# Two transformer blocks in one kernel: PSUM banks of the output products, places of split weights, order of the first splits

## The chip, the cores and the metric

The kernel runs on one core of a Trainium2 chip. The metric is device time in microseconds (us) for one launch: before the change the median of three runs is 2657.95 us (2655.5 to 2659.04). PE is TensorE (matrix products and transposes, which write to PSUM, eight banks of 128 partitions x 512 fp32 numbers), ACT is ScalarE, DVE is VectorE, POOL is GpSimd, and SP is the queue that starts the transfers from memory.

## What is computed

256 tokens of 1024 features go through four mixers, each followed by a gated feed-forward part (FFN): two layers whose mixer has three branches (mLSTM, sparse attention, differential attention), one retention mixer, one short convolution. The last FFN is a mixture of eight experts, two for each token. Cut to the parts that the change touches:

```python
# end of a layer's mixer                              (x2)
merged = gates[0] * (y_a @ w_branch[0]) + gates[1] * (y_b @ w_branch[1]) + gates[2] * (y_c @ w_branch[2])
x = x + merged @ w_out
x = x + (silu(n(x) @ w_gate) * (n(x) @ w_up)) @ w_down
# retention: four heads of 512 values
o = normed(retention(q, k, v));  x = x + (silu(g) * o) @ ret_w_out          # 2048 -> 1024
x = x + swiglu(n(x))                                                       # d_ff = 3584, "the third FFN"
# short convolution
x = x + (B * conv3(C * h)) @ conv_w_out
# experts: top 2 of 8, softmax over the two logits
x = x + sum(gate[:, e] * swiglu_e(n(x)))
out = n(x) * g
```

`n` is an RMS norm. Everything is fp32; the large products are made in fp32r from two parts each.

## The kernel before

**Products in three parts.** For a product in fp32r each operand is split in a high part (a copy rounded to fp32r) and a low part (the operand less its high part). `mm3` adds three matmuls: high x high, high x low, low x high. So each unit of weights (1 MB, 2048 numbers for each partition) that arrives in the ring of six units is read twice: ACT or POOL writes the high part (L1195, L2251), then DVE the low part (L1625, `weights_low`). For the mixers the unit is split in two halves of 1024 numbers (`half_highs` on ACT, `half_lows` on DVE, L1639). Four places hold the split halves, four places of 16 KB (`split_place`) the split units; from the retention mixer on, the halves lie in the memory of split places 0 and 1, and the retention's output inputs in places 2 and 3.

**Banks.** PE takes its PSUM banks from rotating pools, one counter for each pool: `fill(ALL)` goes round all eight, `fill(LOW)` round 0 to 3, `fill(HIGH)` round 4 to 7. `fill` waits until whoever was to empty the bank has done so, at whole banks. Pools overlap, so a bank taken from one pool may still be held by another pool's last user. `give_low` marks a bank that ACT and then DVE must read (the high and the low part of an input).

**Output products.** `to_x_split` (`merged @ w_out`, `o @ ret_w_out`, `y @ conv_w_out`) takes four banks from LOW and adds all its products there, going over 8 or 16 input tiles k. Between them stand transposes of what comes next: `turn_merged` (merged branches), `turn_o` (gated retention output), `turn_residual` (new x, for the FFN). The retention's gates are made by `chunk_split`, which takes two banks from ALL: the halves of a chunk are four steps, then ACT reads both banks with Silu (`v_or_g`). ACT works one chunk ahead in the halves: it makes the fourth half of the next chunk before it empties this chunk's banks. After each of the last three gate chunks, `turn_o(h - 1)` turns one head.

**Starts of the mixers.** `input_split` runs five filler matmuls while the norm is computed, turns the input in four banks from ALL, and runs one more filler (a product that nobody reads) in a bank from LOW, before the first product.

**Orders written by hand.** Nothing is scheduled: PE, ACT, DVE, POOL and SP each run their own list, tied by semaphores. In the third FFN POOL makes the high parts: the first unit when `turn_o(3)` has been read ("o turned"), the others when the new x is complete ("mixed"). DVE's `to_ffn` adds the products to x and makes the low parts of the FFN's inputs.

## Time and profile before

| | |
|---|---|
| Time of three runs, us | 2655.5, 2657.95, 2659.04 |
| The profiled execution, us | 2658.11, its span 2656.3 |
| PE busy | 2592.8 us, 98% of the span |
| DVE, ACT, POOL busy | 68%, 46%, 8% |
| Mean granted clock of PE | 0.994 of full speed |
| Moved by DMA | 610.13 MB, 230 GB/s |

PE is the engine that is busy nearly all the time: the time can fall only where PE waits or runs slowly, and rises by every wait that is added to it. So the profile is read by PE's waits, and for each by what stands around it in order of time. In the rows below a number in square brackets is the idle time of the engine just before the row, and the arrow what ended it; `xN` counts the recorded instructions that a row merges, and each row gives start and length in us.

### The profile page before, as it was taken

The numbers are of one execution on the slowest core, as the hardware profiler recorded it, in microseconds if no ns is written. First come the engines' busy times: TensorE is split into PE (matmuls) and PEld (weight loads), VectorE is DVE, ScalarE is ACT, GpSimd is POOL, SyncE is SP. The second block draws the span as 40 slices with busy tenths as digits, with TensorE's granted clock in tenths as the row PEclk, the third lists the DMA queues.
The fourth block names the chain that finished last, engine by engine and source line by source line (L and its number), as shares of the span: only waits on it lengthen the run. The fifth ranks groups of instructions, "written<-read, shape, count | busy, mean of one in ns | idle before, by whom it ended". The sixth has DMA issues, their size and how long they took to land.

```text
span 2656.3 us, 29239 instructions
## 1 busy us (share of the span) xinstructions
PE 2592.8 (98%) x11620; PEld 1989.4 (75%) x11620; DVE 1803.0 (68%) x1953; ACT 1226.1 (46%) x1423; POOL 218.8 (8%) x104
## 2 busy tenths in 40 slices
PE   8999999999999999999999998999999999999997
PEld 5455578865555888977788897878787888888886
DVE  3754555447445554745655567999999999999996
ACT  2233220023323102363100346777787877777775
POOL 0000023200000332000433100000000000000000
PEclk9999999999999999999999998999999999999999
DMA  6342455534334555545555455999999989999995
GB/s 214 129 154 100 158 192 189 170 110 137 127 113 170 193 190 173 184 157 175 175 190 190 143 176 181 375 325 381 320 379 325 377 324 376 325 355 347 354 345 188
DMA packets 273636, 610.13 MB, mean 230 GB/s; under 512 B 10476, under 2 KB 47522, under 8 KB 273338
## 3 DMA queue, kind: packets, MB, share of 16 engines
q1 hardware_dynamic: 273466, 607.67, 64.6%
q8 instruction: 131, 2.15, 0.3%
q14 instruction: 39, 0.32, 0.0%
HBM read 606.58 MB, written 1.05 MB: 229 GB/s over the span
## 4 chain that ended last, share of the span: by engine, by line
PE 90%; DVE 6%; ACT 3%; issue 1%; DMA 0%; SPq 0%; DVEq 0%; ACTq 0%
PE bank L467 87%; DVE split L1625 4%; PE bank L709 1%; PE bank L497 1%; ACT split L1195 1%; ACT parts L1195 0%; ACT xs L1195 0%; DVE tmp L1674 0%; DVE parts L1686 0%; ACT pbuf L1195 0%; DMA pbuf<-in_gain_rows 0%; DVE parts L1613 0%; ACT L1195 0%; ACT halves L1195 0%; DVE ybuf_tmp_high L1639 0%
## 5 line engine op out<-in xcount | busy, mean ns | idle before, releaser
L467 PE MATMUL bank<-split,parts 128*128 128x512 f32 (+1 forms) x6432 | 1463.3, 388 | 5.7 <-DVE split L1625 3.1
L467 PEld LDWEIGHTS bank<-split,parts 128*128 128x128 f32 x6432 | 1189.4, 188 | 247.3 <-issue 4.0
L1625 DVE TENSOR_TENSOR split<-ring,split 128x2048 fp32r<-128x2048 f32 x444 | 1020.4, 2344 | 81.9 <-POOL split L2251 60.9
L1195 ACT ACTIVATE split<-ring 128x2048 fp32r<-128x2048 f32 x344 | 659.6, 1921 | 187.0 <-PE bank L467 187.0
L467 PE MATMUL bank<-ring,xnT 128*128 128x512 f32 (+2 forms) x896 | 367.6, 567 | 0.0
L2251 POOL TENSOR_SCALAR split<-ring 128x2048 fp32r<-128x2048 f32 x100 | 218.6, 2187 | 1265.2 <-PE bank L467 1035.9
L467 PEld LDWEIGHTS bank<-ring,xnT 128*128 128x128 f32 x896 | 169.4, 190 | 180.0 <-issue 178.9
L1195 ACT ACTIVATE parts<-bank 128x512 fp32r<-128x512 f32 x128 | 68.8, 590 | 327.4 <-PE bank L709 327.4
L1639 DVE TENSOR_TENSOR halves<-ring,halves 128x1024 fp32r<-128x1024 f32 x96 | 116.4, 1224 | 84.1 <-ACT halves L1195 83.5
L1195 ACT ACTIVATE halves<-ring 128x1024 fp32r<-128x1024 f32 x96 | 101.3, 1059 | 153.9 <-PE bank L467 153.9
L1686 DVE TENSOR_TENSOR parts<-bank,parts 128x512 fp32r<-128x512 f32 x128 | 82.4, 686 | 124.9 <-ACT parts L1195 124.9
L1195 ACT ACTIVATE z<-bank 128x512 f32<-128x512 f32 (+2 forms) x52 | 29.6, 568 | 234.2 <-PE bank L467 234.2
L467 PEld LDWEIGHTS bank<-xparts,halves 128*128 128x128 f32 x960 | 115.5, 190 | 2.1 <-ACT xparts L1195 1.6
L467 PE MATMUL bank<-xparts,halves 128*128 128x256 f32 x960 | 116.1, 284 | 0.8 <-DVE xparts L1613 0.8
L1676 DVE SCALAR_TENSOR_TENSOR tmp<-bank,xsum,tmp 128x512 f32<-128x512 f32 (+1 forms) x38 | 27.5, 723 | 110.9 <-PE bank L467 110.9
L1195 ACT ACTIVATE tmp<-bank,xsum 128x512 f32<-128x512 f32 (+1 forms) x38 | 25.3, 667 | 141.6 <-PE bank L467 141.5
L467 PE MATMUL bank<-halves,xparts 128*128 128x512 f32 x384 | 88.6, 391 | 0.0
L467 PE MATMUL bank<-ring,ybuf 128*128 128x512 f32 x192 | 84.1, 594 | 3.5 <-ACT ybuf L1195 3.5
L467 PEld LDWEIGHTS bank<-halves,xparts 128*128 128x128 f32 x384 | 71.8, 188 | 15.1 <-issue 0.5
L1660 DVE TENSOR_TENSOR x_resid<-bank,x_resid 128x512 f32<-128x512 f32 x60 | 41.1, 691 | 51.1 <-PE bank L467 51.1
L1674 DVE TENSOR_TENSOR tmp<-bank,tmp 128x512 f32<-128x512 f32 x112 | 72.6, 685 | 0.2
L467 PEld LDWEIGHTS bank<-ring,ybuf 128*128 128x128 f32 x192 | 35.8, 190 | 46.5 <-issue 42.1
(260 smaller groups left out, 1861.1 us busy)
## 6 DMA issues: line engine op xcount, KB each, us to landing
ring<-in_moe_w_gate SPq DMA_DIRECT2D x112, 1024.0 KB, 8.0
ring<-in_moe_w_up SPq DMA_DIRECT2D x112, 1024.0 KB, 7.5
ring<-in_moe_w_down SPq DMA_DIRECT2D x112, 1024.0 KB, 7.5
ring<-in_w_gate_up SPq DMA_DIRECT2D x44, 1024.0 KB, 5.8
ring<-in_w_in SPq DMA_DIRECT2D x40, 1024.0 KB, 7.1
ring<-in_ret_w_in SPq DMA_DIRECT2D x24, 1024.0 KB, 5.1
ring<-in_w_down SPq DMA_DIRECT2D x22, 1024.0 KB, 5.1
ring<-in_w_in SPq DMA_DIRECT2D x20, 880.0 KB, 6.5
```

What stands on the lines that cost most here:

```text
L467: return nc.tensor.matmul(o, l, r, start=first, stop=final, **kw)
L497: ins = nc.tensor.transpose(bank[b][:, i * P:i * P + rows], src_of(i), ident[0:rows, 0:rows])
L709: return [nc.tensor.transpose(bank[b[tt]][:, f * P:(f + 1) * P], hb[:, tt, f * P:(f + 1) * P], ident) for f in range(n // P)]
L1195: return nc.scalar.activation(out, in_, func, **kw)
L1625: V.tensor_tensor(split[:, split_place(m), 1, :], ring[:, n % RING, :], split[:, split_place(m), 0, :].bitcast(F32), ALU.subtract).then_in ...
L1639: V.tensor_tensor(low, half_of(n, j, by_column), high.bitcast(F32), ALU.subtract).then_inc(half_low.sem, half_low.tick())
L1660: ins = V.tensor_tensor(o, b[:, :], o, ALU.add)
L1674: ins = V.tensor_tensor(hb[:, tt, 0:n], b[:, 0:n], sg[:, tt, 0:n], ALU.mult)
L1676: ins = V.scalar_tensor_tensor(hb[:, tt, 0:n], b[:, 0:n], xsum[:, 3, tt:tt + 1], sg[:, tt, 0:n], ALU.mult, ALU.mult)
L1686: V.tensor_tensor(low, b[:, 0:n].rearrange("p (f t) -> p f t", t=P), high.bitcast(F32), ALU.subtract).then_inc(hidden_low.sem, 1)
L2251: nc.gpsimd.tensor_scalar(split[:, split_place(m), 0, :], ring[:, n % RING, :], 1.0, 0.0, ALU.mult, ALU.add).then_inc(high_made.sem, high_ ...
```

## The change

It has five parts. (1) Pools: `turn_merged(0)` takes its banks from LOW (was ALL), the four products of the third branch from HIGH (was ALL), every `turn_o` from HIGH (was ALL, but for the last). (2) Places: the second unit of the third FFN goes to place 0, whose halves are moved by two so that the last two halves of the retention lie in place 1; POOL makes that unit's high part as soon as two halves before the last two are read, and DVE makes the low part between the second pair of additions and the second half's input lows, instead of behind them. (3) At the end of a layer the halves and the FFN's first units are made in the order 2 halves, unit, half, unit, half, unit, unit, instead of one by one. (4) Three filler matmuls stand ahead of the last expert's `combine`. (5) Since the pools' counters advance differently, later banks from ALL and HIGH are others than before, also in code that the diff does not touch.

```diff
--- before
+++ after
@@ -44,6 +44,7 @@
 LAYER_HALVES = DEPTH * KT
+RET_HALVES = 8 * 2 + 8 * 4 + 2 * KT
 EARLY = 4
@@ -337,12 +338,17 @@
+        def half_place(h):
+            return (h if h < LAYER_HALVES + RET_HALVES else h + 2) % HALVES
         def place_half(h, by_column):
...
             else:
-                whole = [halves[:, h % HALVES, i, :] for i in range(2)]
+                whole = [halves[:, half_place(h), i, :] for i in range(2)]
             return [w.rearrange("p (k c) -> p k c", k=KT) for w in whole] if by_column else whole
@@ -370,7 +376,7 @@
                 return m % SPLITS
-            return (3, 2, 0, 1)[(m - (DEPTH * layer_splits if m < dense_splits else dense_splits)) % SPLITS]
+            return (3, 0, 1, 2)[(m - (DEPTH * layer_splits if m < dense_splits else dense_splits)) % SPLITS]
@@ -417,8 +423,8 @@
-                half_free.extend(split_read[max(m for m in range(n_split[0]) if split_place(m) == h // 2)]
-                                 for h in range(HALVES))
+                half_free.extend(split_read[max(m for m in range(n_split[0]) if split_place(m) == half_place(h) // 2)]
+                                 for h in range(n_half[0], n_half[0] + HALVES))
@@ -862,7 +868,7 @@
                     eng.wait_ge(mrg_dve.sem, pe.next(mrg_dve))
-                    turn_input(xs, (2 * h, 2 * h + 1), HIGH if h else ALL)
+                    turn_input(xs, (2 * h, 2 * h + 1), HIGH if h else LOW)
@@ -871,7 +877,7 @@
                                 turn_merged(0)
-                            b = fill(ALL)
+                            b = fill(HIGH if br == 2 else ALL)
                             for k in range(4):
@@ -1037,11 +1043,11 @@
-            def turn_o(h, pool=ALL):
+            def turn_o(h):
...
                 for fp in (2 * h, 2 * h + 1):
-                    transposes(lambda i: rv[:, i % 2, (2 * fp + i // 2) * P:(2 * fp + i // 2 + 1) * P], 4, "act", pool)
+                    transposes(lambda i: rv[:, i % 2, (2 * fp + i // 2) * P:(2 * fp + i // 2 + 1) * P], 4, "act", HIGH)
                     point("input")
@@ -1053,7 +1059,7 @@
                 if k == 4:
-                    turn_o(RH - 1, HIGH)
+                    turn_o(RH - 1)
                     point("o turned")
@@ -1135,6 +1141,7 @@
+                filler(3 if ends else 0)
                 eng.wait_ge(act_freed.sem, pe.point("y", act_freed))
@@ -1445,9 +1452,10 @@
                     half_highs(1)
-                for _ in range(EARLY):
-                    half_highs(1)
+                for n in (2, 1, 1):
+                    half_highs(n)
                     expert_high(1, layer_splits * li)
+                expert_high(EARLY - 3, layer_splits * li)
                 nth_split[0] += layer_splits - EARLY
@@ -1661,9 +1669,10 @@
-            def to_ffn(gain):
+            def to_ffn(gain, units=0):
                 for h in range(2):
                     add_to_x(BY_HALF[2 * h:2 * h + 2])
+                    weights_low(units if h else 0)
                     lows(gain, pairs=(2 * h, 2 * h + 1))
@@ -2051,9 +2060,10 @@
                 half_lows(1)
-                for _ in range(4):
-                    half_lows(1)
+                for n in (2, 1, 1):
+                    half_lows(n)
                     weights_low(1)
+                weights_low(EARLY - 3)
                 to_ffn(G_FFN + 8 * li)
@@ -2128,8 +2138,7 @@
             weights_low(1)
-            to_ffn(G_FFN0)
-            weights_low(1)
+            to_ffn(G_FFN0, 1)
             norm_inverse()
@@ -2257,8 +2266,12 @@
             weights_high(1, first)
+            for h in range(LAYER_HALVES + RET_HALVES - HALVES, LAYER_HALVES + RET_HALVES - 2):
+                sig, value = half_read[h]
+                eng.wait_ge(sig.sem, value)
+            weights_high(1, first)
             eng.wait_ge(dve_freed.sem, pool.point("mixed", dve_freed))
-            weights_high(units_of(groups2) - 1, first)
+            weights_high(units_of(groups2) - 2, first)
```

**Retention, the end of the second gate chunk on PE** (before, then changed; each row is the line, the instruction, its bank and operands, the size, what it waits for and how many like it; `halves,xparts` are the chunk's products, `const,ret_v` the transposes of `turn_o(0)`, and the rows after them the next chunk).

```order
L467 MATMUL bank7<-halves,xparts 128x512 [waits half_unit_low]
L467 MATMUL bank7<-halves,xparts 128x512 x5
L467 MATMUL bank0<-halves,xparts 128x512 x6
L497 MATMUL bank1<-const,ret_v 128x128 [waits act_emptied,retention_scaled]
L497 MATMUL bank1<-const,ret_v 128x128 x3
L497 MATMUL bank2<-const,ret_v 128x128 [waits act_emptied]
L497 MATMUL bank2<-const,ret_v 128x128 x3
L467 MATMUL bank3<-halves,xparts 128x512 [waits half_unit_low,act_emptied]
L467 MATMUL bank3<-halves,xparts 128x512 x5
```

Changed:

```order
L473 MATMUL bank3<-halves,xparts 128x512 [waits half_unit_low]
L473 MATMUL bank3<-halves,xparts 128x512 x5
L473 MATMUL bank4<-halves,xparts 128x512 x6
L503 MATMUL bank4<-const,ret_v 128x128 [waits act_emptied,retention_scaled]
L503 MATMUL bank4<-const,ret_v 128x128 x3
L503 MATMUL bank5<-const,ret_v 128x128 [waits act_emptied]
L503 MATMUL bank5<-const,ret_v 128x128 x3
L473 MATMUL bank5<-halves,xparts 128x512 [waits act_emptied,half_unit_low,inputs_low]
L473 MATMUL bank5<-halves,xparts 128x512 x5
```

Before, the transposes stood in banks 1 and 2, with nothing of the chunks around them. Now their first bank is 4, the chunk's second, and the next chunk's first bank is 5, which holds the second set of transposes. At `turn_o(1)` it is the same with banks 6 and 7. Behind `turn_o(2)` the output product used to take banks 0 to 3 with the transposes in 1 and 2; now they are in 4 and 5.

**Start of the retention mixer on PE** (`const 128x512` is filler, `const,xs` are the transposes of the input, `xparts,halves` the first product).

```order
L497 MATMUL bank6<-const,xs 128x128 [waits dve_emptied]
L497 MATMUL bank6<-const,xs 128x128 x3
L497 MATMUL bank7<-const,xs 128x128 [waits dve_emptied]
L497 MATMUL bank7<-const,xs 128x128 x3
L497 MATMUL bank0<-const,xs 128x128 [waits hidden_low,act_emptied]
L497 MATMUL bank0<-const,xs 128x128 x3
L467 MATMUL bank3<-const 128x512 [waits dve_emptied]
L467 MATMUL bank1<-xparts,halves 128x256 [waits half_unit_low,inputs_low,hidden_low,act_emptied]
L467 MATMUL bank1<-xparts,halves 128x256 x5
```

Changed:

```order
L503 MATMUL bank1<-const,xs 128x128 x3
L503 MATMUL bank2<-const,xs 128x128 x4
L503 MATMUL bank3<-const,xs 128x128 [waits dve_emptied]
L503 MATMUL bank3<-const,xs 128x128 x3
L503 MATMUL bank4<-const,xs 128x128 [waits dve_emptied]
L503 MATMUL bank4<-const,xs 128x128 x3
L473 MATMUL bank3<-const 128x512 [waits inputs_low,act_emptied]
L473 MATMUL bank5<-xparts,halves 128x256 [waits inputs_low,half_unit_low,dve_emptied]
L473 MATMUL bank5<-xparts,halves 128x256 x5
```

The filler's bank is 3 in both, but the transposes have moved from 5, 6, 7, 0 to 1, 2, 3, 4, so that the filler now waits for the third set. At the start of the convolution they move from 3, 4, 5, 6 to 1, 2, 3, 4 with the same filler in bank 3.

**Third FFN's start on DVE** (`x_resid` are the additions to x, `parts` the low parts of the FFN's input, `split` a unit's low part).

```order
L1660 TENSOR_TENSOR x_resid<-bank2,x_resid 128x512 [waits bank_for_dve]
L1660 TENSOR_TENSOR x_resid<-bank3,x_resid 128x512 [waits bank_for_dve]
L1613 SCALAR_TENSOR_TENSOR parts<-bank4,gcol,parts 128x256 [waits act_emptied,dve_emptied]
L1613 SCALAR_TENSOR_TENSOR parts<-bank4,gcol,parts 128x256
L1613 SCALAR_TENSOR_TENSOR parts<-bank5,gcol,parts 128x256 [waits act_emptied]
L1613 SCALAR_TENSOR_TENSOR parts<-bank5,gcol,parts 128x256
L1625 TENSOR_TENSOR split<-ring,split 128x2048 [waits weights_high]
L1577 TENSOR_TENSOR xsum<-xhalf 128x2 [waits squares_summed]
L1568 TENSOR_SCALAR xsum<-xsum 128x2 [waits dve_step]
L1573 RECIPROCAL xsum<-xsum 128x2 [waits root]
```

Changed:

```order
L1668 TENSOR_TENSOR x_resid<-bank2,x_resid 128x512 [waits bank_for_dve]
L1668 TENSOR_TENSOR x_resid<-bank3,x_resid 128x512 [waits bank_for_dve]
L1633 TENSOR_TENSOR split<-ring,split 128x2048 [waits weights_high,dve_emptied]
L1621 SCALAR_TENSOR_TENSOR parts<-bank6,gcol,parts 128x256 [waits act_emptied]
L1621 SCALAR_TENSOR_TENSOR parts<-bank6,gcol,parts 128x256
L1621 SCALAR_TENSOR_TENSOR parts<-bank7,gcol,parts 128x256 [waits act_emptied]
L1621 SCALAR_TENSOR_TENSOR parts<-bank7,gcol,parts 128x256
L1585 TENSOR_TENSOR xsum<-xhalf 128x2 [waits squares_summed]
L1576 TENSOR_SCALAR xsum<-xsum 128x2 [waits dve_step]
L1581 RECIPROCAL xsum<-xsum 128x2 [waits root]
```

The second unit's low part has moved up past the four instructions that make the input's low parts.

## Rows read from the trace of the kernel before

**Rows 1.** Page, part 1: busy time, share of span, instructions.
```profile
PE 2592.8 (98%) x11620; PEld 1989.4 (75%) x11620; DVE 1803.0 (68%) x1953; ACT 1226.1 (46%) x1423; POOL 218.8 (8%) x104
```

**Rows 2.** PE's waits over the span: us in total, times, longest.
```profile
PE bank L467 <- DVE oT_low L2118: 3.5, 1, 3.5
...
PE bank L467 <- DVE split L1625: 3.1, 1, 3.1
...
PE bank L467 <- DVE oT_high L1639: 1.5, 2, 0.8
PE bank L467 <- DVE tmp L2015: 1.2, 1, 1.2
...
PE bank L497 <- DVE x_resid L1660: 0.9, 1, 0.9
```

**Rows 3.** Timeline, PE, from the retention's second gate chunk.
```profile
1188.72 1.04 PE L497 MATMUL bank<-const,ret_v 128*128 128x128 f32 x8
1189.52 11.16 PE L467 MATMUL bank<-halves,xparts 128*128 128x512 f32 x48
1200.52 1.03 PE L497 MATMUL bank<-const,ret_v 128*128 128x128 f32 x8
...
1212.29 1.03 PE L497 MATMUL bank<-const,ret_v 128*128 128x128 f32 x8
1216.86 0.70 PE L467 MATMUL bank<-halves,oT_high 128*128 128x512 f32 x2 [3.53 <-DVE oT_low L2118]
```

**Rows 4.** Timeline, ACT and DVE, the same stretch.
```profile
1191.35 1.09 ACT L1195 ACTIVATE ret_gate<-bank 128x512 f32<-128x512 f32 x2
...
1201.74 1.07 ACT L1195 ACTIVATE ret_gate<-bank 128x512 f32<-128x512 f32 x2
...
1214.47 1.09 ACT L1195 ACTIVATE oT_high<-bank 128x512 fp32r<-128x512 f32 x2
1215.10 1.29 DVE L2118 TENSOR_TENSOR oT_low<-bank,oT_high 128x512 fp32r<-128x512 f32 x2 [0.24 <-ACT oT_high L1195]
```

**Rows 5.** Timeline, all engines: fillers, and two mixers' starts (1057, 1509 us).
```profile
532.91 4.46 PE L467 MATMUL bank<-const 128*128 128x512 f32 x10
...
1057.94 1.97 PE L497 MATMUL bank<-const,xs 128*128 128x128 f32 x16
...
1060.54 3.23 DVE L1613 SCALAR_TENSOR_TENSOR xparts<-bank,gcol,xparts 128x256 fp32r<-128x256 f32 x8 [0.78 <-ACT xparts L1195]
...
1064.90 1.06 ACT L1195 ACTIVATE halves<-ring 128x1024 fp32r<-128x1024 f32 x1 [2.20 <-PE bank L467]
1067.78 1.06 ACT L1195 ACTIVATE halves<-ring 128x1024 fp32r<-128x1024 f32 x1 [1.82 <-PE bank L467]
...
1509.21 1.97 PE L497 MATMUL bank<-const,xs 128*128 128x128 f32 x16
...
1516.91 1.06 ACT L1195 ACTIVATE halves<-ring 128x1024 fp32r<-128x1024 f32 x1 [2.94 <-PE bank L467]
```

**Rows 6.** Timeline, third FFN's start, DVE and PE.
```profile
1263.21 1.28 DVE L1660 TENSOR_TENSOR x_resid<-bank,x_resid 128x512 f32<-128x512 f32 x2
...
1268.64 3.71 DVE L1625 TENSOR_TENSOR split<-ring,split 128x2048 fp32r<-128x2048 f32 x1
...
1272.40 18.24 PE L467 MATMUL bank<-split,parts 128*128 128x512 f32 x72 [3.13 <-DVE split L1625]
```

**Rows 7.** Stretches: length, busy (x) of PE, PEld, DVE, ACT, POOL, clock.
```profile
1216.00:1220.00 4.00, 3.14 (x14) 2.62 (x15) 1.71 (x3) 0.05 (x1) 0.00 (x0) 1.00 0.68 253
...
1272.40:1276.00 3.60, 3.60 (x10) 2.83 (x11) 3.26 (x4) 0.20 (x1) 1.71 (x1) 0.59 0.65 197
```

**Rows 8.** Timeline, PE and DVE, the last product of the experts.
```profile
2640.74 5.40 PE L467 MATMUL bank<-xnT,ckvT 128*128 128x512 f32 x8 [2.59 <-ACT xnT L1195]
2641.90 0.69 DVE L1660 TENSOR_TENSOR x_resid<-bank,x_resid 128x512 f32<-128x512 f32 x1 [9.81 <-PE bank L467]
...
2646.18 0.69 DVE L1660 TENSOR_TENSOR x_resid<-bank,x_resid 128x512 f32<-128x512 f32 x1 [0.20 <-PE bank L467]
```

## The prediction, made before the changed kernel was run

> **What bounds the kernel now.** I read first the busy times: PE works 2592.8 of 2656.3 us, no other engine over 68% [rows 1]. So the time is PE's instructions plus PE's waits, and the second view is the list of those waits [rows 2]. The reader is to see there that the waits that can be removed are small and single: 3.5 us for a bank of the retention's output product, 3.1 us for a unit of the third FFN, 1.2 us once and 0.8 us twice at the ends of the layers, 0.9 us ahead of the router. Third, the stretches of order in time around these places, on PE and on whoever ends the wait [rows 3 to 6, 8]. Last, the granted clock, because an idle PE can cost more than its idle time: the stretch behind the 3.13 us wait ran at 0.59 of full speed, that is partly at 1.2 instead of 2.4 GHz, while behind the 3.53 us wait it stayed at 1.00, 2.4 GHz throughout [rows 7].
>
> All sums go against the profiled execution, 2658.11 us (span 2656.3 and 1.8 around it), which is 0.16 above the median of the runs. An effect of 0.2%, 5.3 us, is about what a measurement of this kernel tells from no change.
>
> **The removed waits, one by one.**
>
> *Retention's output product.* The transposes start at 1212.29 and the product at 1216.86, 4.57 later, behind the low parts read from banks 1 and 2 [rows 3, 4]. With the transposes in 4 and 5 only bank 0 is in the way, the second bank of the third gate chunk. ACT empties such a pair late, since the next chunk's half comes first: 1201.74 + 1.07 = 1202.81, which is 2.29 behind that chunk's end at 1200.52 [rows 3, 4]. So the product starts some 2.29 + 0.3 behind 1212.29, at 1214.9: **-2.0**.
>
> *Third FFN's second unit.* PE waits 3.13 for the low part at 1268.64, which took 3.71 beside POOL [rows 6]. The additions are over at 1263.21 + 1.28 = 1264.49; the low part now stands right behind them with its high part already there, so even at 3.71 it is done at 1268.2, before PE wants it (1272.40 - 3.13 = 1269.27). The input's low parts, which it is put ahead of, would end at 1268.64 and may now end near 1269.9; PE takes them pair by pair and needs the last one only after it has begun, so I count nothing, at worst 1. The wait of 3.1 goes, and with it the slow clock: the 72 matmuls from 1272.40 took 18.24 us, while at the pitch of an undisturbed chunk (1200.52 - 1189.52 = 11.0 us for 48 of the same size, 0.229 each) they take 16.5, 1.8 less [rows 3, 6]. Together **-5.0** (between -3.1 and -5.2; -1 worse if the input is late).
>
> *Ends of the two layers.* The first output product waits 1.2 for a bank of the third branch, in one layer only (the count is 1, since in the other layer that last bank is outside 0 to 3) [rows 2]; that goes. The 0.8 for the last half goes in both, but DVE has to make the same four units and five halves before it can add to x, and the pairing only puts a half ahead of a unit that ACT could have made sooner. I take half of 0.8 for each layer, between 0 and 0.8: **-1.2 - 0.8 = -2.0**.
>
> *Router.* The late transposes used bank 3 first, which is emptied by the last of four additions: 0.9 us of wait [rows 2]. They now start in bank 1, emptied with the first half, so two of the four sets are made during that wait: **-0.8** (0 to -1).
>
> *Last combine.* PE waits 2.59 there for ACT, and the four additions to x end their products' stretch 2646.18 - 2641.90 = 4.28 apart for three products [rows 8]. A product at full speed takes 0.89, as a filler does (4.46 for five) [rows 5], so three are 2.7 and the slow clock cost 1.6. Three fillers take 2.67, as long as the wait: **-1.5** (0 to -1.6; +0.1 if the clock falls anyway).
>
> The sum of what is removed: 2.0 + 5.0 + 2.0 + 0.8 + 1.5 = **-11.3**.
>
> **What is added.** The order of PE shows two banks in the way that the diff does not name, for ALL and HIGH overlap.
>
> *After the second gate chunk.* The transposes of `turn_o(0)` want bank 4, the chunk's second. ACT empties it at 1191.35 + 1.09 = 1192.44 [rows 4], so they start at about 1192.6 instead of 1188.72. The next chunk wants bank 5, the second set of these transposes, which ACT and DVE must both read. From the start of the transposes: half of their 1.03 and 0.1 until ACT can start, 0.63 from ACT's start to DVE's, 1.29 for the two low parts, 0.3 until PE goes on (0.47 in rows 3 and 4: 1216.86 against 1215.10 + 1.29) [rows 3, 4], together 2.8. So the chunk starts at 1195.4, not at 1189.52: **+5.9**. *After the third* (banks 6 and 7): emptied at 1202.81, transposes at 1203.0, next chunk at 1205.8, against 1200.52 + 0.80: **+4.5**. Queued behind these waits on PE is all its work; ACT and DVE have made the next chunk's four halves by then and can't go further, since the places are full. The chunk itself then runs at its old pace, so nothing is given back. The bounds of both together are +8.5 (no handover cost) and +11.5 (0.47 and more at each).
>
> *Starts of the retention and the convolution.* The filler in bank 3 now waits for the third pair of input low parts. These start 2.60 behind the transposes (1060.54 - 1057.94) and take 3.23 for four pairs, so the third is done at 2.60 + 2.42 = 5.02 [rows 5]. Filler from 5.2 to 6.1, then the first half-tile, 2.88 (the pitch of ACT's halves, 1067.78 - 1064.90), and 0.25 to ACT: 9.2 behind the transposes. Before it was 1064.90 - 1057.94 = 6.96 in the retention and 1516.91 - 1509.21 = 7.70 in the convolution, whose filler waited for the first pair already [rows 5]. So **+2.3** and **+1.5**.
>
> *Clock.* Four long idle stretches of PE arise: 3.9 us (then 1.0 of transposes and 1.8 idle again), 2.5 us (and again 1.8), and 3.2 us at the start of each of the two mixers. What one costs beyond itself the trace bounds by three rows: 1.8 behind 3.13 us, 1.6 behind 2.59, 0 behind 3.53 [rows 6 to 8]. I take their mean, 1.1, for each: **+4.5**, between 0 and 7.2.
>
> On that place the Trainium skill has a rule ("TensorE: Matmul & The Clock Gate", section "What's actually happening"): PE's default is 1.2 GHz, and it is activity that keeps the gate open, so an idle stretch is followed by slow matmuls. Two of the three rows agree, the one with 3.53 us and clock 1.00 does not. By the rule alone all four stretches would be followed by slow matmuls.
>
> Added: 5.9 + 4.5 + 2.3 + 1.5 + 4.5 = **+18.7**. All else keeps its work: the experts' loop has the same rows but for bank and place numbers, whose waits are one turn of a pool behind as before. The sum is 18.7 - 11.3 = +7.4, and 2658.1 + 7.4 = **2665.5**.
>
> **Rivals.**
>
> *A. The clock stays at 2.4 GHz in all four new idle stretches* (not slower, by what can be measured). For it: the longest idle stretch of the trace was followed by full speed [rows 7]; transposes and fillers stand near each of the four. Against: two shorter ones were not. Then +7.4 - 4.5 = +2.9: 2661.0. It decides as long as fewer than about half of the stretches cost their 1.1 to 1.8: below +2.4 for the clock the whole is under 5.3 us. Chance 0.30.
>
> *B. Every stretch is followed by slow matmuls*, at 1.8 each: +7.2 for the clock, +10.1 in all: 2668.2. For it: the rows with 3.13 and 2.59; the second and third boundaries have two idle parts, one behind the other. Against: 3.53. It is the nearest neighbour of the forecast. Chance 0.17. This is what the rule above would give.
>
> *C. The bank waits do not arise in time*, because ACT has emptied the chunk's banks sooner than in these rows; then the gains stand alone: -11.3 and, with the mixers' starts as before, 2646.8. For it only that the change claims separate banks. Against: order and rows say that ACT takes 2.3 to 3.7 us for it, and PE is there 0 us behind the chunk's end. Chance 0.03.
>
> *D. The third FFN gains nothing*, since DVE's low part, moved ahead of the input's, beside POOL's passes delays the input by as much: +3.1 and +1.8 against the forecast, 2670.4. For it: three of POOL's passes run beside DVE there, and the 3.71 us of that low part may be the mark of it [rows 6]. Against: 1 us of delay is what the rows make of it. Chance 0.05.
>
> **How the numbers follow.** The forecast, two or three of the four stretches slow, has 0.45. Its own range is 2662.5 to 2667.5. With A and B, which hold another 0.47, the range is 2659 to 2670; outside lie C, most of D and the ends of the unknown costs. Slower by over 0.2% (above 2663.4): most of the forecast's 0.45, B and D, 0.62. Within 0.2%: A and the forecast's low end, 0.35. Faster by over 0.2%: C, 0.03.
>
> **What would show each step right or wrong.** On PE in the retention: transposes of `turn_o(0)` with an idle time of 3.5 to 4 ended by ACT's Silu, and the next chunk 1.5 to 2 idle behind them, ended by DVE's `oT_low`; the same with 2.3 and 1.8 at `turn_o(1)`; and the output product with some 1.4 in place of 3.53. At both mixers' starts a filler with over 3 us of idle time, ended by DVE's `xparts`. In the third FFN no wait for the second unit and clock 1.00. Ahead of the last combine no idle time and four additions 0.9 apart. The granted clock of the stretches behind the new waits tells A, B and the forecast apart. The prediction is wrong if the new bank waits are missing or under 7 us together, if the third FFN still waits, or if a stretch in the experts' loop differs, where I see no reason for it.

## The result, and the profile after

| | before | after |
|---|---|---|
| Median, us (runs) | 2657.59 (6) | 2666.76 (6) |
| Range of the runs, us | 2655.50 to 2659.93 | 2665.12 to 2668.49 |
| The profiled execution, its span, us | 2658.11, 2656.3 | 2666.89, 2665.1 |
| Mean granted clock of PE | 0.994 | 0.992 |

The ratio is 1.0032, 95% interval 1.0020 to 1.0044: the change makes the kernel slower by 0.3%, which is small, but its interval leaves 1 out. The forecast was 2665.5. In the changed kernel the lines of PE's helper have moved by 6, the others by 6 to 10.

PE's part of the page's busy times, which answers to [rows 1], shows that the 8.8 us are not all waiting: PE is busy 6.4 us longer (2599.2 against 2592.8) for three fillers (2.7 us) and otherwise the same products. The other 3.7 are slow matmuls: some 7.2 us more behind the new waits, 3.4 less in the third FFN and the combine. (A filler shows as two records, as every 128x512 f32 product of its kind does: three fillers are x6.)

```profile
PE 2599.2 (98%) x11626; PEld 1994.0 (75%) x11626; DVE 1805.2 (68%) x1953; ACT 1226.8 (46%) x1423; POOL 219.7 (8%) x104
```

PE's waits after (us in total, times, longest), to be laid beside [rows 2]: the waits for `oT_low`, `split`, `oT_high` by DVE, `tmp` of line 2015 and `x_resid` are gone, and in their place stand waits for banks.

```profile
PE bank L473 <- DVE xparts L1621: 6.4, 2, 3.2
PE bank L503 <- ACT ret_gate L1202: 6.0, 2, 3.7
...
PE bank L473 <- ACT oT_high L1202: 3.2, 2, 1.6
...
PE bank L473 <- ACT ret_gate L1202: 1.3, 1, 1.3
```

The retention's boundaries on PE, in order of time (start, length; in brackets the idle time before and what ended it), where [rows 3] had no idle time until 3.53:

```profile
1192.13 1.07 PE L503 MATMUL bank<-const,ret_v 128*128 128x128 f32 x8 [3.69 <-ACT ret_gate L1202]
1194.82 13.61 PE L473 MATMUL bank<-halves,xparts 128*128 128x512 f32 x48 [1.62 <-ACT oT_high L1202]
1210.71 1.06 PE L503 MATMUL bank<-const,ret_v 128*128 128x128 f32 x8 [2.27 <-ACT ret_gate L1202]
1213.39 12.77 PE L473 MATMUL bank<-halves,xparts 128*128 128x512 f32 x48 [1.62 <-ACT oT_high L1202]
1226.00 1.03 PE L503 MATMUL bank<-const,ret_v 128*128 128x128 f32 x8
1228.34 0.73 PE L473 MATMUL bank<-halves,oT_high 128*128 128x512 f32 x2 [1.31 <-ACT ret_gate L1202]
```

To be seen: the second idle stretch is 1.62 each time, and the 48 products behind take 13.61 and 12.77 us, where they took 11.16 and 11.14. ACT and DVE beside it, which answer to [rows 4]:

```profile
1190.91 1.08 ACT L1202 ACTIVATE ret_gate<-bank 128x512 f32<-128x512 f32 x2
1192.80 1.08 ACT L1202 ACTIVATE oT_high<-bank 128x512 fp32r<-128x512 f32 x2 [0.81 <-PE bank L503]
```
```profile
1193.43 1.29 DVE L2128 TENSOR_TENSOR oT_low<-bank,oT_high 128x512 fp32r<-128x512 f32 x2 [2.58 <-ACT oT_high L1202]
```

ACT reads the chunk's banks until 1191.99, and PE starts 0.14 later; DVE's low parts end at 1194.72, and PE starts 0.10 later. The row names ACT's `oT_high` as what ended the wait, but ACT had read its last at 1193.88, 0.94 before PE went on; the one that came last is DVE's `oT_low`, as predicted. The handover costs less than the 0.3 that I had put in.

The starts of the two mixers, PE and then ACT, which answer to [rows 5]:

```profile
1053.73 1.97 PE L503 MATMUL bank<-const,xs 128*128 128x128 f32 x16
1058.91 1.10 PE L473 MATMUL bank<-const 128*128 128x512 f32 x2 [3.22 <-DVE xparts L1621]
...
1515.87 1.97 PE L503 MATMUL bank<-const,xs 128*128 128x128 f32 x16
1521.05 2.04 PE L473 MATMUL bank<-const 128*128 128x512 f32 x2 [3.22 <-DVE xparts L1621]
```
```profile
1064.47 1.06 ACT L1202 ACTIVATE halves<-ring 128x1024 fp32r<-128x1024 f32 x1 [5.98 <-PE bank L473]
...
1526.69 1.06 ACT L1202 ACTIVATE halves<-ring 128x1024 fp32r<-128x1024 f32 x1 [6.07 <-PE bank L473]
```

The filler starts 5.18 behind the transposes in both (I had 5.2), and the first half follows at 10.74 and 10.82 instead of 9.2. The stretches of the timeline behind the new waits (length; busy of PE, PEld, DVE, ACT, POOL; granted clock, share of the transfers, GB/s), with the third FFN last, to be read with [rows 7]:

```profile
1058.90:1063.00 4.10, 4.09 (x19) 3.62 (x20) 2.92 (x4) 0.00 (x0) 0.00 (x0) 0.65 0.29 97
1194.80:1198.40 3.60, 3.58 (x9) 2.83 (x10) 1.24 (x2) 0.00 (x0) 0.00 (x0) 0.50 0.09 38
1213.39:1217.00 3.61, 3.61 (x9) 2.83 (x10) 1.22 (x2) 0.00 (x0) 0.00 (x0) 0.55 0.53 218
1521.05:1524.50 3.45, 3.45 (x10) 2.42 (x11) 2.91 (x4) 0.00 (x0) 0.00 (x0) 0.52 0.32 109
1277.70:1281.30 3.60, 3.60 (x19) 2.99 (x18) 3.39 (x7) 2.77 (x5) 3.60 (x2) 1.00 0.51 121
```

The first four are at 1.2 GHz for the larger part or throughout (9 products in 3.6 us, not 17 as at full speed), the third FFN is at 2.4 GHz. There DVE's low part of the unit, now ahead of the input's, takes 2.29 and no longer 3.71, against [rows 6]:

```profile
1276.02 2.29 DVE L1633 TENSOR_TENSOR split<-ring,split 128x2048 fp32r<-128x2048 f32 x1
1278.50 1.66 DVE L1621 SCALAR_TENSOR_TENSOR parts<-bank,gcol,parts 128x256 fp32r<-128x256 f32 x4 [0.18 <-ACT parts L1202]
```

The last products of the experts, PE and DVE, which answer to [rows 8]: no wait, and the four additions are 2.58 apart from first to last (they were 4.28).

```profile
2648.28 2.74 PE L473 MATMUL bank<-const 128*128 128x512 f32 x6
2651.28 3.70 PE L473 MATMUL bank<-xnT,ckvT 128*128 128x512 f32 x8 [0.26 <-issue]
```
```profile
2652.44 0.69 DVE L1668 TENSOR_TENSOR x_resid<-bank,x_resid 128x512 f32<-128x512 f32 x1 [10.06 <-PE bank L473]
...
2655.02 0.69 DVE L1668 TENSOR_TENSOR x_resid<-bank,x_resid 128x512 f32<-128x512 f32 x1 [0.17 <-PE bank L473]
```

**Where the 8.78 us went**, by how far the same instruction of the two timelines lies apart at the borders of each stage:

| Stage | predicted | measured |
|---|---|---|
| ends of the two layers | -2.0 | -2.06 and -0.67 |
| retention's start: wait, clock | +2.3, + | +2.24, +1.53 |
| second boundary: waits, clock | +5.9, + | +5.74, +2.45 |
| third boundary: waits, clock | +4.5, + | +4.33, +1.63 |
| output product | -2.0 | -2.23 |
| third FFN | -5.0 | -4.85 |
| convolution's start: wait, clock | +1.5, + | +1.51, +1.61 |
| late transposes | -0.8 | -0.87 |
| last combine | -1.5 | -1.45 |
| clock, the four together | +4.5 | +7.22 |
| sum | +7.4 | +8.9 |

The clock's share of a start is what the first half comes later than 9.2 behind the transposes; that of a boundary is the chunk's length over 11.16 or 11.14. The sums take the clock from its own row. Beside these stand two differences in stretches that the change doesn't touch: -1.4 in the first layer's first products and +1.6 in the first expert's first products. With them the sum is 9.1; some 0.3 of the difference to 8.78 lies in no single place. The prediction named a differing stretch in the experts' loop as a sign of being wrong. But the wait ahead of it is the same 2.08 in both, and the changed kernel's e3 and e6, with the same program there, have the short time; so it is no effect of the change. More on both below.

### The profile page after: what moved, and what is told of

It is laid out like the page before. It is cut to its first block, busy times and chain, and to the rows that moved or that the text cites. A ratio compares the mean times of both kernels' runs of the same rounds, so it can differ in the third digit from the quotient of the medians.

```text
span 2665.1 us, 29255 instructions
## 1 busy us (share of the span) xinstructions
PE 2599.2 (98%) x11626; PEld 1994.0 (75%) x11626; DVE 1805.2 (68%) x1953; ACT 1226.8 (46%) x1423; POOL 219.7 (8%) x104
## 4 chain that ended last, share of the span: by engine, by line
PE 90%; DVE 6%; ACT 3%; issue 1%; DMA 0%; SPq 0%; DVEq 0%; ACTq 0%
PE bank L473 87%; DVE split L1633 3%; PE bank L715 1%; PE bank L503 1%; ACT split L1202 1%; ACT xs L1202 0%; ACT parts L1202 0%; DVE tmp L1683 0%; DVE parts L1695 0%; ACT halves L1202 0%; DMA pbuf<-in_gain_rows 0%; ACT pbuf L1202 0%; ACT L1202 0%; DVE x_resid L1668 0%; DVE xparts L1621 0%
```

## Experiments

Each ratio is against runs of the kernel before on the same chip, whose median was 2659.56 for e1 to e4, 2657.74 for e5 to e8 and 2660.08 for e9 to e11. Against the changed kernel's 1.0032 a step of 0.001 is 2.7 us.

**e1: banks of chunks and transposes apart.** All other banks stay as in the changed kernel.

```diff
             for h in range(1, RH):
-                chunk_split("act")
+                chunk_split("act", ((0, 1), (2, 3), (6, 7))[h - 1])
...
-                    transposes(..., 4, "act", HIGH)
+                    transposes(..., 4, "act", ((4, 5), (6, 7))[h // (RH - 1)])
```

> The changed kernel, but the retention's last three gate chunks and the transposes between them have banks that never meet: chunks in 0 and 1, 2 and 3, 6 and 7; transposes in 4 and 5 three times, then 6 and 7. All other banks stay. My theory (the new waits are bank waits, and the slow matmuls behind them come from the idle time): the two boundaries lose their waits, 5.7 and 4.3 us, and the slow clock, 2.45 and 1.63, and the output product, which now waits for no bank, starts 0.8 behind its transposes instead of 2.34: 1.5. Sum -15.7, from 2666.9 to 2651.2. Rival one (the matmuls behind the waits are slow for another reason, such as the transfers that run there): the waits and the product alone, -11.6, 2655.3. Rival two (ACT or DVE is behind there anyway, and another wait takes the place of the bank's): the idle stretches stay with another name and the time falls by under 5, to over 2662.

Measured: 2651.30 us, ratio 0.9970 (0.9960 to 0.9980). PE's timeline at the boundaries of e1:

```profile
1187.20 1.04 PE L509 MATMUL bank<-const,ret_v 128*128 128x128 f32 x8
1187.99 11.16 PE L479 MATMUL bank<-halves,xparts 128*128 128x512 f32 x48
1199.00 1.03 PE L509 MATMUL bank<-const,ret_v 128*128 128x128 f32 x8
1199.79 11.14 PE L479 MATMUL bank<-halves,xparts 128*128 128x512 f32 x48
1210.77 1.03 PE L509 MATMUL bank<-const,ret_v 128*128 128x128 f32 x8
1211.56 0.71 PE L479 MATMUL bank<-halves,oT_high 128*128 128x512 f32 x2
```

By the ratios that is 0.0062 or 16.5 us below the changed kernel; the theory has 15.7, rival one 11.6, rival two under 5. From the retention's transposes (1052.48 in e1, 1053.73 after) to the output product it is 159.08 us against 174.61: -15.5. Two things of 1.5 us cancel in it: the retention's start kept its clock here by chance, and the second chunk waits 1.39 for the scalar engine, in banks 0 and 1 (e9 takes that up). The boundaries' own waits are gone and none takes their place, so the changed kernel paid those 14 us for bank numbers alone, and the 3.53 us of the kernel before could be won as well.

**e2: the filler at the mixers' starts in another bank.**

```diff
-                filler(1)
+                b = ALL[(turn[ALL] + 2) % 8]
+                free_bank(b)
+                turn[LOW] = turn.get(LOW, 0) + 1
+                mm(bank[b][:, :], ident, const[:, 0:HALF], True, True)
```

> The changed kernel, but the filler behind the input's transposes of the retention and the convolution goes to bank 7, which none of these transposes uses (it was bank 3, the third set's). My theory: the first half in each mixer comes as early as in the retention of the kernel before, 6.96 behind the transposes, instead of 10.74 and 10.82: -3.8 and -3.9, together -7.6 to -7.7, 2659.3; of these some 1.5 each is the slow clock behind the wait. Rival (the clock falls anyway, since the low parts of the input are not earlier): only the waits, 2.2 each, go, -4.5, 2662.4. Rival two (the first product waits for the same low parts as long as the filler did): nothing, 2666.9.

Measured: 2660.04 us, ratio 1.0005 (0.9997 to 1.0014), 0.0027 or 7.2 us below the changed kernel's. The first halves in ACT's timeline come 6.95 and 6.96 behind the transposes (1053.57 and 1512.71):

```profile
1060.52 1.06 ACT L1205 ACTIVATE halves<-ring 128x1024 fp32r<-128x1024 f32 x1 [2.19 <-PE bank L473]
```
```profile
1519.67 1.06 ACT L1205 ACTIVATE halves<-ring 128x1024 fp32r<-128x1024 f32 x1 [2.20 <-PE bank L473]
```

That is -3.8 and -3.9, as expected; both rivals fall. The filler waits no more (it starts 1.80 behind the transposes), and the clock stays at 1.00 in both. In the convolution this is 0.7 better than before the change.

**e3: fillers in the boundaries' waits.** The bank waits stay, PE works in them.

```diff
             def turn_o(h):
+                if h < 2:
+                    warm(2, 4 if h == 0 else 2)
                 eng.wait_ge(rets_dve.sem, pe.next(rets_dve))
...
+                if h < 2:
+                    warm(2, 2)
```

> The changed kernel with filler matmuls in bank 2, which is free there, laid into the four idle stretches at the retention's two boundaries: 4 ahead of the first transposes (3.57 us of work in 3.69 idle), 2 behind them (1.78 in 1.62), 2 and 2 at the second boundary (1.78 in 2.27, 1.78 in 1.62). The bank waits stay as they are. My theory (the slow matmuls come from the idle time): the two chunks behind run at their old pace, 11.1 us instead of 13.6 and 12.8, and the fillers come out some 0.3 late: -3.7, 2663.2. Rival (the chunks are slow for the transfers, or for another reason that idle time has no part in): +0.3, 2667.2.

Measured: 2661.91 us, ratio 1.0022 (1.0005 to 1.0040). One of the twelve runs took 2690.22 us at a mean clock of 0.945 (the others 2660.39 to 2664.95, at 0.993 to 0.995); no trace of it was kept, and its cause is open. It lifts the ratio and widens the interval: the mean of the other eleven is 2662.5, 1.0013 of the kernel before, some 5 us below the changed kernel, where the theory has 3.7 below it and the rival 0.3 above. With that run in, the times do not tell the two apart; the timeline of PE and the stretches do:

```profile
1197.00 11.14 PE L478 MATMUL bank<-halves,xparts 128*128 128x512 f32 x48
1207.98 1.88 PE L478 MATMUL bank<-const 128*128 128x512 f32 x4
1210.41 1.06 PE L508 MATMUL bank<-const,ret_v 128*128 128x128 f32 x8 [0.55 <-ACT ret_gate L1211]
1211.31 1.88 PE L478 MATMUL bank<-const 128*128 128x512 f32 x4
1213.10 11.14 PE L478 MATMUL bank<-halves,xparts 128*128 128x512 f32 x48
```
```profile
1197.00:1200.60 3.60, 3.60 (x17) 3.01 (x17) 1.22 (x2) 0.53 (x1) 0.00 (x0) 1.00 0.09 35
1213.10:1216.70 3.60, 3.60 (x17) 3.00 (x17) 1.21 (x2) 0.53 (x1) 0.00 (x0) 1.00 0.50 204
```

Both chunks take 11.14, at a clock of 1.00, with the same transfers beside them (shares 0.09 and 0.50; after, 0.09 and 0.53). From the retention's transposes to the output product it is 170.52 us against 174.61, -4.1. So the 4.08 us that the two chunks took too long are the price of idle time, not of traffic. The fall is shown to come from PE standing still at these two places.

**e4: e1 and e2 together.**

> The changed kernel with the banks of e1 and the filler's bank of e2 together. My theory (the causes are apart and add up): -15.7 - 7.6 = -23.3, 2643.6, that is 14.5 below the kernel before. Rival (what is won at the mixers' starts is lost again at the next wait, as the halves' loading or the recurrent values behind set the pace): 2648 to 2651.

Measured: 2644.02 us, ratio 0.9941 (0.9928 to 0.9954), 0.6% below the kernel before. Against the changed kernel that is -0.0091, where e1 has -0.0062 and e2 -0.0027: the causes add up. In the trace the first halves come 6.96 and 6.95 behind the transposes, and the boundaries have no wait.

**e5: the kernel before with the third FFN's second unit alone.**

```diff
-            to_ffn(G_FFN0)
-            weights_low(1)
+            to_ffn(G_FFN0, 1)
```

and with it the places, the halves' shift and POOL's early pass, as in the change.

> The kernel before with one part of the change alone: the second unit of the third FFN in place 0, its high part made early by the third engine's early pass and its low part between the second additions and the input's low parts. My theory: the 3.13 us wait and the slow clock behind it (1.8) go, -4.9, 2653.3, a little under 0.2% faster. Rival (the low parts of the input, which now come behind the unit's, are late by what was won): the wait goes over to them, and the gain is under 2, over 2656. Rival two (the wait goes, the slow clock comes anyway, since the idle time was not its cause): -3.1, 2655.0.

Measured: 2655.08 us, ratio 0.9988 (0.9979 to 0.9997), 3.2 us below the kernel before. The time by itself is that of rival two (2655.0) as much as of the theory; the trace has to decide. From DVE's additions to `x` to the FFN's second transposes the trace has 29.04 us where the kernel before has 33.28 (1258.42 to 1287.46; 1258.21 to 1291.49): -4.2. The 3.13 us wait and its slow clock are gone (1.00 from 1262 to 1286.5), so both rivals fall; 0.52 us of wait stays for the next unit:

```profile
1266.49 8.43 PE L471 MATMUL bank<-split,parts 128*128 128x512 f32 x36
1275.45 11.17 PE L471 MATMUL bank<-split,parts 128*128 128x512 f32 x48 [0.52 <-DVE split L1629]
```

Ahead of that next unit's low part two tiny DVE instructions are long, which in the changed kernel take 0.15 and 1.76:

```profile
1268.79 1.87 DVE L1581 TENSOR_TENSOR xsum<-xhalf 128x2 f32<-128x2 f32 x1
1270.69 1.85 DVE L1572 TENSOR_SCALAR xsum<-xsum 128x2 f32<-128x2 f32 x1
```

**e6: the old order of halves and units at the layers' ends.**

```diff
-                for n in (2, 1, 1):
-                    half_highs(n)
-                    expert_high(1, layer_splits * li)
-                expert_high(EARLY - 3, layer_splits * li)
+                for _ in range(EARLY):
+                    half_highs(1)
+                    expert_high(1, layer_splits * li)
```

and the same on DVE.

> The changed kernel with the old order of the halves and units at the ends of the two layers (half, unit, four times over). What the trace of the changed kernel says against my prediction's size of 0.4 a layer: the wait for the last half comes back whole, 0.77 in both layers, and nothing else, +1.55 in all. By the prediction's reasoning (DVE sets the pace there, so the pairing wins half): +0.8 in all, with the products at the layers' ends 0.4 later each. Rival (another half's wait takes its place): 0.

Measured: one execution, 2667.33 us. In PE's list of waits the wait for the last half is back in both layers:

```profile
PE bank L473 <- DVE oT_high L1646: 1.6, 2, 0.8
```

ACT's squares of `x` at the layers' ends, whose distance from the stage's start is compared, come 0.66 and 0.63 later than in the changed kernel. Pairing was worth 1.3 of the 1.55 that the waits hold, not the 0.8 of my prediction. This rests on one trace; a single time tells nothing of 1.3 us.

**e7: e4 with fillers in the router's waits.**

```diff
+            warm(3)
             eng.wait_ge(mask_dve.sem, pe.next(mask_dve))
...
+            warm(3)
             big = tokens(0) > P
             gather(big)
+            warm(2)
```

> The kernel of e4 with filler matmuls in bank 7 in three waits of the router's stage, where the granted clock is 0.50: three ahead of the counting products (the wait was 3.03 us), three ahead of the first gather (2.54), two ahead of the first expert's first unit (2.08). My theory (the idle time brings 1.2 GHz): the gather of 32 matmuls takes 4.0 as in later experts, not 6.07, -2.1; the counting products up to -1.1; the first expert's chunk always 11.2, which in the runs so far took 11.2 or 12.8, -0.8 in the mean. Sum -3 to -4 from e4, near 2640.5. Rival (these waits sit on the vector and scalar engines' steps, and the fillers are in the way of what is due): +1 to +2, 2645 to 2646.

Measured: 2642.29 us, ratio 0.9939 (0.9926 to 0.9953), the same as e4's. The gather is faster, but the fillers ahead of it run slowly and stand in its way:

```profile
1610.97 4.54 PE L479 MATMUL bank<-const 128*128 128x512 f32 x6 [0.91 <-DVE route L2238]
1615.35 3.73 PE L479 MATMUL bank<-ybuf,xs 128*128 128x128 f32 x32
```

Three fillers take 4.54 us here and 2.74 ahead of the combine. From the router's products to the first expert's chunk it is 21.96 us; without fillers it was 20.2 (six traces) or 21.8 (five). The first expert's chunk took 11.2 in this trace and in e8's, as the theory has it, but the theory's sum falls: the gain ahead of it is used up. The rival's loss of 1 to 2 us is not in the times either.

**e8: one filler at the very start.**

```diff
+                if li == 0:
+                    warm(1)
                 norm_transposes(idle=(5, 1) if li else (0, 0))
```

> The kernel of e7 with one filler more, in the 2.56 us wait ahead of the very first transposes. In the six traces so far the first 128 products of the first layer took 27.9 us three times and 29.5 to 30.1 three times, with the same program there. My theory (this is the clock behind the idle start, and it falls out by chance): the filler makes it 27.9 always, -0.9 in the mean from e7. Rival (the start is too short of work for one filler to decide it, or the loads of the weights are what differs): no change, and again both values in the traces.

Measured: 2642.43 us, ratio 0.9940 (0.9926 to 0.9953); the 128 products took 27.86 us in the one trace. Without the filler 27.9 came in 4 of 12 traces, so one trace proves nothing. The transposes ahead of them took 2.77 us, where the other twelve traces have 3.3 to 3.7, so something is won there; but the times show no gain. Open.

**e9 and e10: the second gate chunk's banks.** e9 is e4 with these banks, e10 is e4 again.

```diff
-                chunk_split("act", ((0, 1), (2, 3), (6, 7))[h - 1])
+                chunk_split("act", ((3, 4), (0, 1), (6, 7))[h - 1])
...
-                               ((4, 5), (6, 7))[h // (RH - 1)])
+                               ((5, 6), (2, 3), (4, 5), (6, 7))[h])
```

> The kernel of e4 with other banks for the gate chunks and the transposes: chunks in 3 and 4, 0 and 1, 6 and 7; transposes in 5 and 6, 2 and 3, 4 and 5, 6 and 7. In e4 the second gate chunk took banks 0 and 1, which the retention's own products had used last, and waited 1.39 us for the scalar engine. My theory: banks 3 and 4 are those that were used longest ago, as in the changed kernel, so the wait goes and the chunk ends 1.5 us earlier behind the retention's start (130.9 in the trace of e2, 132.4 in that of e4); nothing else waits: -1.5 from e4, near 2642.5 where e4 has 2644. Rival (the halves of that chunk are not made sooner, since the scalar engine makes them behind its reading of those products): no change from e4, and a wait for half units in place of 1.39.

> The kernel of e4 once more, beside e9 on one chip. Theory and rival of e9 differ by 1.5 us in the difference of these two; for this one alone all expect e4's ratio of 0.994 to the kernel before.

Measured: e9 2644.14 us, ratio 0.9934 (0.9920 to 0.9948); e10 2642.79 us, 0.9934 (0.9921 to 0.9948). The chunk and what follows in e9, then the chunk in e10:

```profile
1175.56 11.46 PE L479 MATMUL bank<-halves,xparts 128*128 128x512 f32 x48
1186.86 1.04 PE L509 MATMUL bank<-const,ret_v 128*128 128x128 f32 x8
```
```profile
1174.10 11.18 PE L479 MATMUL bank<-halves,xparts 128*128 128x512 f32 x48 [1.39 <-ACT tmp L1213]
1185.11 1.04 PE L509 MATMUL bank<-const,ret_v 128*128 128x128 f32 x8
```

The next transposes, with which the chunk ends, start 130.76 and 132.45 behind the input's transposes (1056.10 and 1052.66): -1.7 in the traces, as the theory has it, and no wait takes the place of the 1.39. The times do not tell 1.7 us, with differences of 1.6 us by chance in each execution. e4, e9 and the two with more fillers (e7, e8) are not apart, all 0.6 to 0.7% under the kernel before.

**e11: the changed kernel without the fillers ahead of the combine.**

```diff
-                filler(3 if ends else 0)
```

> The changed kernel without the three filler matmuls ahead of the last expert's combine. My theory (they keep the clock): the 2.59 us wait comes back, the clock behind it is near 0.6, and the four additions to x are 4.3 apart in place of 2.6, +1.5. Rival (the clock had risen anyway, being above that place by chance): additions 2.6 apart, no difference.

Measured: one execution, 2670.37 us. The wait is back, the products take 5.15 instead of 3.70:

```profile
2653.22 5.15 PE L473 MATMUL bank<-xnT,ckvT 128*128 128x512 f32 x8 [2.81 <-ACT xnT L1201]
```

From the last down product (2644.66) to the last addition (2658.41) it is 13.75 us, against 12.33 after: 1.4, the fillers' worth, and all of it in the products (5.15 against 3.70): the wait is as long as the fillers were. The clock in the first 3 us behind the wait is 0.51. The rival falls. The expected 4.3 from the first addition to the last did not come: they are 3.08 apart (2655.33 to 2658.41), since here most of the slow stretch lies ahead of the first addition.

## Why the prediction was right, and where a step was not

- **What is removed.** The sum was 11.3 and is 12.1. The output product (2.0, measured 2.23, with the wait of 1.3 named), the third FFN (5.0, 4.85; e5 alone 4.2), the late transposes and the combine (1.5, 1.45; e11 1.4) came out with the waits gone that were named. Of these, the third FFN, the halves' order and the combine's fillers were tried singly (e5, e6, e11); the third branch's bank in the first layer (1.2) and the router's late transposes are read from the timelines alone. The layers' term was too small: I halved the 0.8 because DVE has to make the same pieces before it can add, but e6 shows that PE's wait for the half was the path, and nearly all of it was won (1.5 of 1.55 in the timelines, 1.3 by e6).
- **The two boundaries.** Bank waits of 5.74 and 4.33 where 5.9 and 4.5 stood; e1 takes them away with bank numbers alone. Rival C (they don't arise) is out. The four waits together, with the starts' below, were 13.8 where 14.2 stood: the handover of 0.3 was too much.
- **The mixers' starts.** 2.24 and 1.51 where 2.3 and 1.5 stood; in e1, whose retention start kept the clock, the first half comes 9.25 behind the transposes (I had 9.2). e2 shows that the filler's bank is the whole cause of both the wait and the slow clock there.
- **The clock.** This term was mis-sized: 4.5 predicted, 7.22 measured. I took the mean of three rows, of which one (3.53 us of idle time, clock 1.00) cost nothing, for each of four stretches; none of the four was free. It is the 7.2 of rival B, and by mechanism B is what happened: every stretch slow. That the forecast lay nearer in time (2665.5, measured 2666.76, B 2668.2) is luck: 0.8 of gains that I had put too low and 0.4 of waits too high stood against 2.7 of clock too low. By the difference from before (+7.4 forecast, +10.1 B, +8.8 in the traces, +9.2 in the medians) B is as near or nearer.
- In the Trainium skill ("TensorE: Matmul & The Clock Gate", section "What's actually happening") the default state of PE's clock is throttled, and activity releases the throttle. The four stretches of the changed kernel agree (clocks 0.50 to 0.65 behind them), and so does e3, where work in the same waits keeps 1.00. Where every stretch is slow, the clock's term is B's 7.2. But one start of e1, with the same 3.22 us of idle time, went on at 1.00, as the 3.53 us did in the kernel before and in e5; the rule tells the direction, the rows a chance.
- **Rival A** (clock stays, 2661.0) is out by the stretches at 0.50 to 0.65, **rival D** (the third FFN gains nothing) by the timeline and e5: the unit's low part took 2.29, and the input's low parts end 4.2 behind the additions, as before (the prediction had allowed 1 us more).

## What to carry to other kernels

- A bank pool that is advanced by a counter gives every other stage new neighbours when one caller leaves it. Print the bank of each fill around the change, and look for a product next to transposes in one bank: here that cost 14 us in one stage, and other bank numbers alone brought the changed kernel down by 0.9%, some 24 us by the ratios (e4; e9 the same within the noise).
- A filler needs a bank whose last reader is long done. Laid into a wait ahead of time, while the clock is still up, it holds the clock for nothing; put in once the clock is down, it runs at half speed and delays what it should help.
- Count a new idle stretch of PE of some 3 us at its length plus 1.5 to 2.9 us for the clock, as in these traces. The retention's boundaries were slow behind their waits in 8 of 8 cases (after, e2, e6, e11: 48 products in 12.68 to 14.01 us instead of 11.15), the mixers' starts in 9 of 10. The 3.53 us of the kernel before and of e5 cost nothing in 2 of 2.

## What the runs showed of the hardware

- **The same wait has two prices.** Behind an idle time of 3.22 us at the mixers' starts the clock fell in 9 of 10 cases (after, e1, e3, e6, e11) and stayed in one. Both are in e1: the first half comes 9.25 behind the transposes in the retention, where the clock is 1.00 behind the wait, and 12.03 in the convolution, where it is 0.50; elsewhere a slow start has 10.74 to 10.85. So a fall costs 1.5 to 2.8 us there. The first expert's first 48 products, behind 2.08 us (e3: 2.22), took 11.2 us in eight traces and 12.8 in three (after, e2, e11), at clocks of 1.00 and 0.50. The three slow ones are those with the longest gather ahead of the wait (6.07 to 6.12 us, against 5.18 to 5.90), though the clock was back at 1.00 in the gather's last microsecond in all eleven. The first layer's first 128 products took 27.9 or 29.5 to 30.1, the router's stretch 20.2 or 21.8. In each case nothing in the program differs there, and each is worth 1.6 to 2.2 us. Three such steps together are 5 us, an estimate of what they can make of the 8.3 us between the kernel before's fastest and slowest of 26 runs on one chip (2653.93 to 2662.19; on another chip it went up to 2665.25). This is why effects under 2 us were read from the timelines here. What decides between the two was not tried.
- **A tiny DVE instruction beside POOL.** The sum over 128x2 values takes 0.15 us in the changed kernel and 1.87 in e5, in both beside POOL's pass over 128x2048. The instruction behind it took 1.85 in e5, 1.76 in the changed kernel and 0.17 in the kernel before. Each long one ends within 0.03 us of the end of a pass of POOL's (in e5 at 1270.65 and 1272.54, POOL's passes at 1270.65 and 1272.52), so a tiny instruction that is held ends with the pass beside it. Where it starts in the pass does not decide: in e5 and in e4 the sum starts 0.04 us behind the pass's start and takes 1.87 and 0.15. What does was not tried.
